# Norm, mix and hand-over code of a two-layer hybrid decoder step rebuilt in three places

## The reference, cut to what matters

```python
h = _rmsnorm(x, lw['g_attn']) * (1 + sc1) + sh1        # per sequence: scale and shift from w_ada
cq, ckv, kr, u, gates = split(h @ lw['w_in'])          # latent queries, keys, pooling branch, gates
...                                                    # attention: prompt causal, samples over 2048 cached rows
mixed = (gate_a * a_out + gate_b * b_out) @ lw['w_out'] # a_out: pooled branch, b_out: attention
x = x + g1 * mixed
h2 = _rmsnorm(x, lw['g_ffn']) * (1 + sc2) + sh2
z, conv_new = _causal_dwconv(h2 @ lw['w_up'], conv_prev, lw['w_conv'], lw['b_conv'])
x = x + g2 * ((jax.nn.silu(zg) * zv) @ lw['w_down'])
```

## Time and profile before

| | us |
|---|---|
| median of 3 runs | 2501.23 (2497.98 to 2507.91) |
| profiled execution, its own time | 2507.76 |
| its span in the trace | 2506.0 |
| PE busy / DVE busy / ACT busy / POOL busy | 2301.7 / 1191.5 / 920.2 / 751.5 |
| mean granted TensorE clock | 0.965 of full |

### The profile page before, as it was taken

How to read it: one execution, slowest core, us unless ns; L and a number is a source line. 1 busy time by engine, 2 the same in 40 slices (tenths; PEclk the granted TensorE clock), 3 DMA queues, 4 the chain that set the end, 5 groups by cost and what they waited for, 6 DMA issues and landing times.

```text
span 2506.0 us, 44003 instructions
## 1 busy us (share of the span) xinstructions
PE 2301.7 (92%) x16385; PEld 2055.9 (82%) x16385; DVE 1191.5 (48%) x1697; ACT 920.2 (37%) x1915; POOL 751.5 (30%) x360
## 2 busy tenths in 40 slices
PE   5999999999987999989969999999999869999896
PEld 3888898766777999989968898976667869999896
DVE  3433560743356566641253507346443666666222
ACT  4223323742223555541132232266222145555222
POOL 1333433400013433323333244332000233333341
PEclk8999999999998999999989999999999989999998
DMA  8364331133311222235336542211332212222221
GB/s 269 121 201 101 76 80 52 30 93 98 93 49 53 67 84 81 78 97 150 106 101 212 155 85 71 81 47 39 94 109 64 63 43 84 81 79 84 68 85 61
DMA packets 336606, 230.62 MB, mean 92 GB/s; under 512 B 62612, under 2 KB 319901, under 8 KB 336436
## 3 DMA queue, kind: packets, MB, share of 16 engines
q1 hardware_dynamic: 334198, 223.20, 31.1%
q10 hardware_dynamic: 2274, 5.60, 0.8%
HBM read 223.15 MB, written 5.60 MB: 91 GB/s over the span
## 4 chain that ended last, share of the span: by engine, by line
PE 72%; issue 13%; DVE 5%; POOL 4%; ACT 2%; DVEq 2%; DMA 1%; SPq 0%; ACTq 0%; POOLq 0%
PE PS L1361 46%; PE PS L1329 6%; PE PS L1678 5%; PE PS L1724 4%; POOL wlo L860 4%; PE PS L1595 2%; PE PS L1621 1%; PE PS L1520 1%; PE PS L1598 1%; PE PS L1409 1%; PE PS L1572 1%; DVE xn L958 1%; DVE xn L954 1%; DVE win L1075 1%; PE PS L1672 1%
## 5 line engine op out<-in xcount | busy, mean ns | idle before, releaser
L860 POOL TENSOR_TENSOR wlo<-raw,whi 128x1024 fp32r<-128x1024 f32 x260 | 633.2, 2437 | 1555.3 <-ACT whi L475 1555.3
L475 ACT ACTIVATE whi<-raw 128x1024 fp32r<-128x1024 f32 x260 | 275.2, 1059 | 917.5 <-PE PS L1361 738.9
L1361 PE MATMUL PS<-h_hi,whi 128*128 128x288 f32 (+1 forms) x2528 | 551.2, 300 | 30.0 <-POOL wlo L860 29.2
L1361 PE MATMUL PS<-h_lo,whi 128*128 128x288 f32 (+1 forms) x2528 | 546.6, 298 | 0.0
L1361 PE MATMUL PS<-h_hi,wlo 128*128 128x288 f32 (+1 forms) x2528 | 546.1, 297 | 0.0
L1361 PEld LDWEIGHTS PS<-h_hi,whi 128*128 128x128 f32 (+1 forms) x2528 | 410.1, 190 | 45.5 <-issue 30.9
L1361 PEld LDWEIGHTS PS<-h_lo,whi 128*128 128x128 f32 (+1 forms) x2528 | 411.5, 190 | 0.7
L1361 PEld LDWEIGHTS PS<-h_hi,wlo 128*128 128x128 f32 (+1 forms) x2528 | 411.3, 189 | 0.7
L1269 DVE TENSOR_SCALAR conv<-zext,convp 128x592 f32<-128x592 f32 x88 | 157.8, 1793 | 153.1 <-ACTq L779 152.9
L1361 PE MATMUL PS<-act_hi,whi 128*128 128x288 f32 x704 | 152.6, 298 | 3.1 <-ACT conv_rows L815 3.1
L969 DVE SCALAR_TENSOR_TENSOR x<-PS,mod,x 128x288 f32<-128x288 f32 (+1 forms) x32 | 16.6, 518 | 285.9 <-PE PS L1361 283.3
(11 more groups left out here) (251 smaller groups left out, 3460.1 us busy)
## 6 DMA issues: line engine op xcount, KB each, us to landing
raw<-w_up SPq DMA_DIRECT2D x88, 512.0 KB, 3.8
pages<-cache_latent SPq DMA_DIRECT2D x256, 144.0 KB, 2.1
raw<-w_in SPq DMA_DIRECT2D x64, 512.0 KB, 4.0
ada_ring<-w_ada SPq DMA_DIRECT2D x64, 512.0 KB, 4.9
raw<-w_down SPq DMA_DIRECT2D x32, 512.0 KB, 3.8
ada_first<-w_ada SPq DMA_DIRECT2D x16, 512.0 KB, 9.8
raw<-w_out SPq DMA_DIRECT2D x16, 512.0 KB, 3.9
ada_next<-w_ada SPq DMA_DIRECT2D x16, 512.0 KB, 3.8
```

Source lines behind the costliest of these rows:

```text
L475: nc.scalar.activation(whi[:, slot], raw[:, slot], ACT.Copy).then_inc(hi_ready.sem, 1)
L860: nc.gpsimd.tensor_tensor(wlo[:, slot], raw[:, slot], whi[:, slot].bitcast(F32), ALU.subtract).then_inc(lo_ready.sem, 1)
L1361: r = mm(PS[0:m, 2 * (j % 2) + half, 0:HT], w, o[:, k0 + k, half * HT:half * HT + HT], start=(first and k == 0 and part is whi and o is xh ...
```

## The change

It rebuilds three things.

**Norm.** PE now sums per token into five columns (`token_sums`), ACT takes the root of 128 by 5 values (`token_root`), DVE the reciprocal of 128 by 5. DVE scales the identity by it (`diag`, five pieces) and PE multiplies a matrix of ones by each (`spread_inverse`), so that the inverse root lies in PSUM for all tokens. DVE multiplies a tile by it and the gain in one instruction (`scale_tile`), ACT adds the shift and rounds (`high_parts`), DVE forms the rest (`low_part`); POOL has no part in it. The samples of all tiles go together, in three instructions and a rest. `first_two` runs the first half of the columns as tiles come and the second half two tiles behind. At the very end the tiles are scaled by `g_final` inside the down loop, and the inverse root is applied per token while the transposed blocks are copied out, by DVE.

**Mix.** The prompt columns' addition of `uext` is done inside the sample attention, one tile after each sequence's scores; ACT rounds (`mixed_high`) and DVE takes the rests (`mixed_low`) of the prompt columns around the last sequence's projection, the samples once in between. That projection now writes bank 6.

**Hand-over and parameters.** The 44 transposes become 7 (`turn_state`), placed ahead of the third down unit, with 2 copies and 14 DMAs by SP at the fifth unit; down asks for its operand tiles eight at a time. The second layer's parameters are loaded at the fifth down unit of the first layer into `rows_next`, transposed after its unit 20 and copied (`parameter_columns`), and `first_gain` is formed before its last residual. In addition the rounding and the subtraction of a unit take only its width (`width`), and POOL's loops over units 2 to 53 and over the down units are written out.

```diff
+    def width(u):
+        if U_KR <= u < U_U:
+            return 128
+        if U_QN <= u < U_POOL:
+            return 768
+        if U_POOL <= u < U_GB and (u - U_POOL) % 3 == 0:
+            return 512
+        return 768 if U_DOWN <= u and (u - U_DOWN) % 3 == 2 else 1024
...
-                sp.wait_ge(x_new.sem, x_new.at(l, 0))
-                for r, (name, n) in zip((P_GA, P_GF, P_PS, P_BA, P_GQ, P_GK), (("g_attn", 8), ("g_ffn", 8), ("pool_scale", 8), ("b_ada", 48), ("g_q", 6), ("g_kv", 2))):
...
+                def parameters(l, rows):
+                    for r, (name, n) in zip((P_GA, P_GF, P_PS, P_BA, P_GQ, P_GK), (("g_attn", 8), ("g_ffn", 8), ("pool_scale", 8), ("b_ada", 48), ("g_q", 6), ("g_kv", 2))):
...
+                if l == 0:
+                    parameters(0, rows)
+                else:
+                    sp.wait_ge(x_new.sem, x_new.at(l, 0))
+                    sp.wait_ge(prev_T.sem, prev_T.at(l, 1))
...
+                    if w == 4:
+                        sp.wait_ge(cl_ev.sem, cl_ev.at(l, 1))
+                        for i in range(7):
+                            n = 7 if i < 2 else 6
+                            for out, a, b in ((O["conv_p"][l, 0], 0, 2), (O["conv_s"][l].rearrange("b r d -> (b r) d"), 2, 2 * NC)):
+                                sp.dma_start(out.rearrange("c (f p) -> c f p", p=128)[:, i:2 * KF:7], conv_rows[18 * i + a:18 * i + b, 0:n, :]).then_inc(cl_out.sem, 16)
...
+                    if l + 1 < DEPTH and w == 4:
+                        sp.wait_ge(act_ready.sem, act_ready.at(l, KF))
+                        sp.wait_ge(cl_T.sem, cl_T.at(l, 1))
+                        parameters(l + 1, rows_next)
...
-                nc.scalar.activation(whi[:, slot], raw[:, slot], ACT.Copy).then_inc(hi_ready.sem, 1)
+                nc.scalar.activation(whi[:, slot, 0:width(u)], raw[:, slot, 0:width(u)], ACT.Copy).then_inc(hi_ready.sem, 1)
...
+            def token_root(l, k):
+                act.wait_ge(ssum_p.sem, ssum_p.at(l, k + 1))
+                nc.scalar.activation(softm[:, 0:5], PS[:, 6, 384:389], ACT.Sqrt, bias=eps[:, 0:1], scale=1.0 / D).then_inc(root.sem, 1)
+            def high_parts(l, k, shift):
+                for f in range(KD):
+                    act.wait_ge(scaled.sem, scaled.at(l, KD * k + f + 1))
+                    nc.scalar.activation(h_hi[:, f, 0:TP], xn[:, f % 4, 0:TP], ACT.Identity, bias=mod[:, shift + f, 0:1], scale=1.0).then_inc(affine.sem, 1)
+                    if f == 1:
+                        act.wait_ge(scaled_s.sem, scaled_s.at(l, k + 1))
+                        nc.scalar.activation(h_hi[:, :, TP:T], xs[:], ACT.Copy).then_inc(affine_s.sem, 1)
...
+                def mixed_high(f):
+                    nc.scalar.activation(h_hi[:, f, 0:TP], gate_b[:, f, 0:TP], ACT.Copy).then_inc(mix_hi.sem, 1)
+                act.wait_ge(spv.sem, spv.at(l, NB))
+                mixed_high(0)
+                mixed_high(1)
                 latent_output(NB - 1)
+                for f in range(2, 6):
+                    mixed_high(f)
+                act.wait_ge(mixed_s.sem, mixed_s.at(l, 1))
+                nc.scalar.activation(h_hi[:, :, TP:T], gate_b[:, :, TP:T], ACT.Copy).then_inc(mix_hi_s.sem, 1)
+                mixed_high(6)
+                mixed_high(7)
...
-                for n in range(11):
-                    act.wait_ge(cl_T.sem, cl_T.at(l, n + 1))
-                    nc.scalar.activation(conv_rows[:, 512 * n:512 * n + 512], PS[0:2 * NC, 4 + n % 4, :], ACT.Copy).then_inc(cl_ev.sem, 1)
-                act.wait_ge(cl_ev.sem, cl_ev.at(l, 11))
-                act.dma_start(O["conv_p"][bass.ds(l, 1)].rearrange("a b r d -> (a b r) d"), conv_rows[0:2, :]).then_inc(cl_out.sem, 16)
-                act.dma_start(O["conv_s"][bass.ds(l, 1)].rearrange("a b r d -> (a b r) d"), conv_rows[2:2 * NC, :]).then_inc(cl_out.sem, 16)
+                def state_rows():
+                    act.wait_ge(cl_T.sem, cl_T.at(l, 1))
+                    nc.scalar.activation(conv_rows[:, 0:4].rearrange("p a b -> p (a b)"), PS[0:126, 4, :], ACT.Copy)
+                    nc.scalar.activation(conv_rows[:, 4:7].rearrange("p a b -> p (a b)"), PS[0:126, 5, 0:384], ACT.Copy).then_inc(cl_ev.sem, 1)
...
+                n = width(u) if isinstance(u, int) else 1024
+                nc.gpsimd.tensor_tensor(wlo[:, slot, 0:n], raw[:, slot, 0:n], whi[:, slot, 0:n].bitcast(F32), ALU.subtract).then_inc(lo_ready.sem, 1)
...
-            def norm_rests(l, k):
...
+            def inverse_tokens(l, k, per_token=False):
+                dve.wait_ge(root.sem, root.at(l, k + 1))
+                last = v.reciprocal(softm[:, 5:10], softm[:, 0:5])
+                if per_token:
+                    last.then_inc(fin_rinv.sem, 1)
+                    return
                 v.drain()
+                for n in (4, 0, 1, 2, 3):
+                    c = 128 * n
+                    w = min(128, T - c)
+                    v.tensor_scalar(diag[:, c:c + w], ident[:, 128 - w:128], softm[:, 5 + n:6 + n], None, ALU.mult).then_inc(diag_set.sem, 1)
             def normalise(l, k, gain, shift):
-                with dve.Fori(0, KD // 4) as i:
-                    for s in range(4):
-                        f = 4 * i + s
-                        dve.wait_ge(h_tile.sem, h_tile.at(l, KD * k + f - 3))
-                        v.tensor_tensor(xn[:, s, :], flat(x[:, bass.ds(f, 1), :]), rinv[:], ALU.mult)
-                        v.drain()
-                        t = by_seq(xn[:, s, TP:T])
-                        v.tensor_tensor(t, t, over_tokens(flat(gain[:, bass.ds(f, 1), 1:NC])), ALU.mult)
-                        v.drain()
-                        v.tensor_tensor(t, t, over_tokens(flat(mod[:, bass.ds(f + shift, 1), 1:NC])), ALU.add).then_inc(scaled.sem, 1)
+                def samples(ap):
+                    return ap.rearrange("p f (b s) -> p f b s", b=NB)
+                def each(ap):
+                    return ap.unsqueeze(3).broadcast_to([128, KD, NB, NS])
+                def scale_tile(f):
+                    v.scalar_tensor_tensor(xn[:, f % 4, 0:TP], x[:, f, 0:TP], gain[:, f, 0:1], PS[:, 7, :], ALU.mult, ALU.mult).then_inc(scaled.sem, 1)
+                def low_part(f):
+                    dve.wait_ge(affine.sem, affine.at(l, KD * k + f + 1))
+                    v.scalar_tensor_tensor(h_lo[:, f, 0:TP], xn[:, f % 4, 0:TP], mod[:, shift + f, 0:1], h_hi[:, f, 0:TP].bitcast(F32), ALU.add, ALU.subtract).then_inc(h_tile.sem, 1)
+                v.tensor_tensor(samples(xs[:]), samples(x[:, :, TP:T]), each(gain[:, :, 1:NC]), ALU.mult)
+                v.drain()
+                dve.wait_ge(rinv_p.sem, rinv_p.at(l, 5 * k + 5))
+                scale_tile(0)
+                scale_tile(1)
+                v.tensor_tensor(xs[:], xs[:], PS[:, 6, 256:256 + TS].unsqueeze(1).broadcast_to([128, KD, TS]), ALU.mult)
+                v.drain()
+                v.tensor_tensor(samples(xs[:]), samples(xs[:]), each(mod[:, shift:shift + KD, 1:NC]), ALU.add).then_inc(scaled_s.sem, 1)
+                low_part(0)
+                scale_tile(2)
+                low_part(1)
+                dve.wait_ge(affine_s.sem, affine_s.at(l, k + 1))
+                v.tensor_tensor(h_lo[:, :, TP:T], xs[:], h_hi[:, :, TP:T].bitcast(F32), ALU.subtract).then_inc(h_samples.sem, 1)
+                for f in range(2, KD):
+                    if f + 1 < KD:
+                        scale_tile(f + 1)
+                    low_part(f)
...
+                    v.tensor_tensor(gate_b[:, b, 0:TP], gate_b[:, b, 0:TP], uext[:, b, 0:TP], ALU.add)
...
+                def mixed_low(f):
+                    dve.wait_ge(mix_hi.sem, mix_hi.at(l, f + 1))
+                    v.tensor_tensor(h_lo[:, f, 0:TP], gate_b[:, f, 0:TP], h_hi[:, f, 0:TP].bitcast(F32), ALU.subtract).then_inc(mix_tile.sem, 1)
+                for f in range(4):
+                    mixed_low(f)
                 dve.wait_ge(uvs.sem, uvs.at(l, 1))
-                v.tensor_tensor(gate_b[:, :, TP:T], gate_b[:, :, TP:T], PS[:, 0, :].rearrange("p (a b) -> p a b", a=KD), ALU.mult)
+                v.tensor_tensor(gate_b[:, :, TP:T], gate_b[:, :, TP:T], PS[:, 6, :].rearrange("p (a b) -> p a b", a=KD), ALU.mult)
                 v.drain()
-                for f in range(KD):
-                    s = f % 2
-                    v.tensor_tensor(tmp[:, s, :], gate_b[:, f, :], uext[:, f, 0:T], ALU.add)
-                    v.drain()
-                    v.tensor_copy(h_hi[:, f, :], tmp[:, s, :])
-                    v.drain()
-                    v.tensor_tensor(h_lo[:, f, :], tmp[:, s, :], h_hi[:, f, :].bitcast(F32), ALU.subtract)
-                    v.drain().then_inc(mix_tile.sem, 1)
+                v.tensor_tensor(gate_b[:, :, TP:T], gate_b[:, :, TP:T], uext[:, :, TP:T], ALU.add).then_inc(mixed_s.sem, 1)
+                mixed_low(4)
+                dve.wait_ge(mix_hi_s.sem, mix_hi_s.at(l, 1))
```

(68 more changed lines are left out.)

204 lines of the change are left out of this document (99 added, 105 removed).

## The result

The changed kernel takes 2430.7 us (median of 4 runs, 2423.1 to 2434.2), beside 2504.6 us for the kernel before on the same chip (2498.0 to 2513.9): a ratio of 0.970 (95% interval 0.966 to 0.974). It is faster by 3.0%, 74 us, as forecast: 2424 was said, 77.4 us of gain. The profiled execution happens to be the fastest of its runs, 2423.1 us with a span of 2421.3, so between the two profiled spans lie 84.7 us. A second series of the same kernel gave 2430.0 us and a profiled span of 2425.8.

What follows compares the result with a forecast made beforehand. PE's work plus its waits and slow stretches were taken as the bound. Gains of 16 + 8.4 + 9 + 10 + 20 + 11.5 + 2.5 = 77.4 us from the median 2501.2 gave 2424 us, range 2402 to 2448.

Steps and rivals of the forecast that it cites:

- moved work: First layer's down loop: transposes, copies and the sixth unit's wait behind SP's DMAs cost PE about 1.1 plus 0.5 us.
- Norm ahead of up: From token sums to the end of up's first two units, each layer: 23.5 instead of 31.6 us, 8 each, 16 in all.
- Mix: After the attention's last projection, each layer: tiles rounded early, first pair ends at 738.8 instead of 743.8, 5 us each.
- Up to down: Between the phases, each layer: down starts 12 us earlier, less transposes and a possible half-clock spell; 10 us each, 20 in all.
- Layer boundary: Between layers: the wait for parameters goes, first pair ends at 1296 instead of 1306.1; 10 us, 8.4 net of moved work.
- Start: Kernel start to the end of the first pair: ends at 67 instead of 76, 9 us gained (6 to 12).
- End: After the last down phase: first block copied at 2482.2 instead of 2494.0, 11.5 us gained.
- Narrow units: Query and pool units: less POOL and ACT work cuts PE's waits for `wlo` by 2.5 us (0 to 6).
- The clock takes part back: Rival: PE drops to half rate after shortened waits in all seven rebuilt stretches, costing 18 us, 2442 in all; chance 0.15.
- More gain: Rival: less idling keeps PE at full clock in following stretches, a sixth of some 85 us gained, 2410; chance 0.15.
- Not covered: Rival: attention has no room for the additions (11 us) and the sixth down unit waits for DMAs (3 more), 2438; chance 0.1.
- Slower by late fetching: Rival: POOL's written-out loops are fetched late, so `wlo` is late for PE; 2698 at 4.5 us a unit; chance 0.03.

Runs made afterwards that it cites:

- add_more: Changed kernel with three more DVE operations of the addition's size behind each addition in the sample attention; 2451.9 us, ratio 0.980 to the kernel before.
- wide_inverse: Changed kernel with the four layer norms' inverse root made wide again, without diagonal pieces or spreading matmuls; 2437.5 us, ratio 0.972 to the kernel before.
- down_waits: Changed kernel with down waiting for all 22 operand tiles and the seven transposes ahead of its first unit; 2443.6 us, ratio 0.974 to the kernel before.
- mix_serial: Changed kernel with its old mix put back: DVE adds, rounds and takes rests after the projection; 2443.5 us, ratio 0.975 to the kernel before.
- keep_busy: Changed kernel with matmuls that serve nothing in PE's waits around the norms; 2424.2 us, ratio 0.969 to the kernel before.
- early_lo: Changed kernel with ACT rounding the next layer's first two units before the boundary's root; 2428.3 us, ratio 0.971 to the kernel before.
- wide_units: Changed kernel with all units rounded at the full width of 1024 again, POOL's loops still written out; 2436.4 us, ratio 0.971 to the kernel before.
- wide_loops: Changed kernel with all units at full width and POOL's units in engine loops again; 2433.8 us, ratio 0.970 to the kernel before.
- best: Changed kernel plus four edits: first unit runs ahead, early rounding at the boundary and ahead of up, filler matmuls at up norms and end; 2401.0 us, ratio 0.959 to before.
- whole_tiles: Changed kernel with PE taking both halves of a tile together in the first two units; 2441.8 us, ratio 0.976 to the kernel before.
- add_behind: Changed kernel with only the prompt columns' addition moved out of the attention, behind the last sequence; 2431.1 us, ratio 0.971 to the kernel before.

## Why the prediction was right, step by step

**The sum.** 77.4 us were forecast, 74 came by the medians and 84.7 between the profiled spans. These two differ because the profiled execution of the kernel before lies 3.2 us above its median (2507.8 against 2504.6), and that of the changed kernel 7.6 below (2423.1 against 2430.7). By the ledger, all places but the stretch from the first pair to the projection gained 75.7 us (74.6 in the second series), where the forecast without the narrow units had 74.9. Part of that hit is luck: the mix brought 4 us more than said, the end 2.1 less, boundary and moved work 0.9 less, and these nearly cancel. The long stretch became 9.6 us shorter in the first layer of one profile and 6.2 in the other, and 0.6 longer in the second layer; 5.0 and 5.3 of it are the wait for `uext`, and the rest is mostly PE's busy time at a clock that differs between executions (granted clock in the first layer 0.98 before, 1.00 and 0.99 after). The forecast had 2.5 us for it.

**Norm ahead of up: 8 each said, 7.7 measured, by other numbers.** The step "I take 1.3 for the token sums" failed: 2.29 us. The sums run at half clock here, as the two wide ones did, and at one clock five with one moving column take what two with 288 take: 2.29 and 2.29 us at the lower, 1.28 and 1.24 at the full one. 1.3 is the price at full clock. "The spreading matmuls end about 0.6 later" failed by 1.2. The time came back in the pair: 12.8 + 2.5 + 0.5 were said and 14.5 measured, as DVE paces tiles at 1.32 us, not 1.45, and PE's slow spell lies inside that. (The second layer's stretch, read as 36.6 us before, is 37.3 between PE's marks; no term hangs on it.)

**Mix: 5 each said, 7.0 measured** (8.6 and 8.9 against the mix put back). The failing step is "1.9 for the clock": the pair follows the projection without a gap and has a clock of 1.00, so 1.9 were charged for nothing. "Attention additions at cost nothing" holds.

**Up to down: 12 less 2 said, 11.8 less 0.9 measured in the first layer and 11.8 less 2.3 in the second.** The other gain is as read: the early start. "A half-clock spell that today falls into the idle part may cost 1.2" came true in the second layer alone, in both profiles: down starts and the next matmuls run at half rate,

```profile
2257.15 0.71 PE L1447 MATMUL PS<-act_hi,whi 128*128 128x288 f32 x2 [2.14 <-ACT zext L827]
2257.66 0.68 PE L1447 MATMUL PS<-act_lo,whi 128*128 128x288 f32 x2
```

with a granted clock of 0.52 in the first 3.4 us of the phase. In add_more, after the same wait of 2.14 us, the second pair of matmuls takes 0.43 us. The phase is 143.3 us long in the nine profiles with this spell and 141.8 in the three without it, so the spell costs 1.5; the seven transposes are the other 0.93. In the first layer no spell follows in either profile of the changed kernel.

**Layer boundary: 10 said, 9.3 measured; moved work 1.6 said, 1.8 measured** (down in the first layer grew by 2.7, of which 0.93 are the seven transposes). "The samples' gain waits once" was right (2.85 instead of 0.68), and what was called the poorer case was right too: the diagonal pieces took 3.17 us instead of 1.04. By the Trainium skill, SBUF — State Buffer, section "Who interferes with whom", `tensor_scalar` can hold the ports that DVE shares with GpSimd; the trace agrees, with 2.1 us here. The section also says that an instruction with one SBUF input outside those modes does not contend; the 3.75 us reciprocal beside POOL in wide_inverse agrees. So the first tile came 12.5 us after the sums began, not 10.8, and the pair gave 1.0 back (14.8 instead of 15.8). That the wait for the parameters is what the boundary gained is read from the rows; no run puts their late loading back. The sixth down unit: its wait was put at 0.5, bounds 0 to 2. It is 0.7 and 0.6 us in the two profiles, and 0.4 to 2.6 over all thirteen with these 27 DMAs ahead of the load. Down in the first layer is 156.0 to 157.7 us where the wait is at most 0.7, and 158.6 to 161.1 where it is 1.4 or more (157.2 in down_waits, which has seven transposes fewer inside). Each of these longer phases also has a half-clock spell, but not always behind the wait: in mix_serial, add_more, wide_inverse, keep_busy and early_lo it stands at the start of down, in wide_units and wide_loops (waits of 2.6 and 2.0 us) behind the wait, in best at both. whole_tiles has the spell at the start and a wait of 0.5 only, in 157.7 us. Why the wait is mostly longer where the spell comes first was not settled. That these 27 DMAs cause the wait is read from their place ahead of the load; taking them elsewhere was not tried.

**Start: 9 said, 8.9 and 7.8 measured.** **End: 11.5 said, 9.4 measured**; token sums again, and 40 transposes that begin at half clock: the first block is copied 4.1 us after the sums began, not 2.6, and first to fifth take 8.2, not 7.8. keep_busy gives 1.9 of it back.

**Narrow units: 2.5 said for `wlo`, 0 measured there, up to 5.3 at `uext`.** The mechanism was wrong, found by wide_units. How much of the 5.3 reaches the time is not shown: with wide units the second layer's long stretch, which has the wait, is 2.7 us longer than in the changed kernel, and the first layer's, which has none, 3.9 to 7.3.

**The rivals.** *The clock takes part back*: the granted clock in the rebuilt stretches is 0.75 to 1.00, not lower than before in any of them, and fillers brought 1.2 us per norm; it did not come. The one spell more, at the start of the second layer's down, costs 1.5 us, and the forecast had counted 1.2 for it. The Trainium skill, TensorE: Matmul & The Clock Gate, section on HAM oscillation, expects waits between bursts to put the array back each time. The trace agrees behind some pairs (after 2.91 us of waiting in the out phase two matmuls take 0.68 to 0.74 us for seven such pairs, and 0.43 only after them) and not behind others (0.53, then 0.43, after 2.92 us in add_behind); and where it agrees, a slow PE can hide behind DVE. *More gain*: only the profiled execution comes near it, and that one lies 7.6 us below its median. *Not covered*: the additions cost nothing; the sixth unit's wait is 0.4 to 2.6 us. *Slower by late fetching*: wide_loops shows no such cost.

## What to carry to other kernels

Split a first use so that the part that is ready late (here the samples, the second half) is asked for late, and let one of two parallel units run ahead, so that its successor's preparation hides behind the other. The first was worth 2 to 4 us a place here, the second took 2 us off each of six waits and some half clock with it. When DVE and GpSimd both read SBUF, try moving the GpSimd instruction by one step: at the boundary that brought 1.5 us, where the shorter inverse root had brought 0.4. And before paying to keep PE's clock up, see whether PE is the one that sets the pace.

## What the runs showed of the hardware

- Five fp32 matmuls with one moving column and 128 columns of weights took 2.29 us at the lower clock and 1.28 at the full one (keep_busy); two with 288 columns took 2.26 to 2.29 and 1.24.
- A DVE `tensor_scalar` from SBUF to SBUF and a `tensor_tensor` with two SBUF operands sat out a GpSimd instruction (3.17 instead of 1.04 us for five, of which the last alone took 2.41; 2.85 instead of 0.68); a reciprocal of 128x576 with one SBUF operand did not (3.75 us in both cases, with 2.8 us of GpSimd's work beside it in one).
- Whether the clock falls after a wait of 2.9 us is not fixed by the wait, nor by PE's work right before it: after 2.9 us in the out phase the next matmuls ran at half rate in the changed kernel, in both series and both layers, and at full rate in add_more, with the same instructions there. After 1.0 us in the same place they did not run at half rate (best, both layers). The same holds for 2.14 us ahead of the second layer's down: half rate behind it in the changed kernel, full rate in add_more. Why was not settled. Such a spell costs 1.3 to 2.7 us.
